# Six of the expert loads split by rows: 112 rows and twice 8 rows in place of 128

## The reference, cut to what matters

```python
def expert_block(args):
    xb, e = args
    gate, up = jnp.split(xb @ w_gate_up[e], 2, axis=-1)
    return (jax.nn.silu(gate) * up) @ w_down[e]
```

## Time and profile before

| | before |
|---|---|
| device time, median of 3 runs | 1189.67 us (1188.84 to 1191.55) |
| device time of the profiled execution | 1190.5 us |
| its span | 1189.2 us |
| PE busy | 1054.2 us, 89% |
| VectorE, ScalarE, GpSimd busy | 576.2, 479.2, 86.5 us |
| moved by DMA | 330.31 MB, mean 278 GB/s |

### The profile page before, as it was taken

How to read it: one execution, slowest core, us unless ns; L and a number is a source line. 1 busy time by engine, 2 the same in 40 slices (tenths; PEclk the granted TensorE clock), 3 DMA queues, 4 the chain that set the end, 5 groups by cost and what they waited for, 6 DMA issues and landing times.

```text
span 1189.2 us, 21996 instructions
## 1 busy us (share of the span) xinstructions
PE 1054.2 (89%) x9608; PEld 861.8 (72%) x9608; DVE 576.2 (48%) x843; ACT 479.2 (40%) x652; POOL 86.5 (7%) x91
## 2 busy tenths in 40 slices
PE   9999999996676665566678999999999999999998
PEld 8889998663333333333324899999999999999986
DVE  6765777441212121212124676664454548666643
ACT  6655953221111111111124743443357765544433
POOL 0621001000000000000000400000210004000000
PEclk9999999998778889888887999999999999999999
DMA  9843589999999999999999576454534235665520
GB/s 364 320 165 137 188 325 420 401 419 428 427 428 425 427 428 427 427 428 415 429 425 382 174 233 209 156 185 160 190 111 144 90 107 186 222 212 182 183 97 35
DMA packets 104222, 330.31 MB, mean 278 GB/s; under 512 B 4339, under 2 KB 76332, under 8 KB 86334
## 3 DMA queue, kind: packets, MB, share of 16 engines
q1 hardware_dynamic: 102064, 322.77, 70.3%
q10 hardware_dynamic: 1470, 4.02, 0.9%
q0 software_dynamic: 592, 2.10, 0.5%
HBM read 327.82 MB, written 1.06 MB: 277 GB/s over the span
## 4 chain that ended last, share of the span: by engine, by line
PE 66%; DMA 29%; DVE 2%; ACT 2%; issue 1%; SPq 0%; DVEq 0%; ACTq 0%
DMA wide<-in_w_gate_up_dram 18%; PE PS L489 13%; PE PS L490 13%; PE PS L491 13%; DMA wide<-in_w_down_dram 11%; PE PS L1229 5%; PE PS L858 4%; PE PS L504 2%; PE PS L852 2%; PE PS L505 2%; PE PS L506 2%; PE PS L1385 1%; PE PS L838 1%; DMA raw<-in_w_in_dram 1%; PE PS L1162 1%
## 5 line engine op out<-in xcount | busy, mean ns | idle before, releaser
L1992 DVE TENSOR_TENSOR lo<-raw,hi 128x2048 fp32r<-128x2048 f32 (+1 forms) x111 | 253.2, 2285 | 147.3 <-ACT hi L1477 118.8
L1477 ACT CAST hi<-raw 128x2048 fp32r<-128x2048 f32 (+1 forms) x109 | 204.0, 1875 | 111.1 <-PE PS L491 74.3
L489 PE MATMUL PS<-AH,hi 128*128 128x256 f32 (+1 forms) x816 | 232.3, 285 | 1.0 <-DVE AL L2496 1.0
L490 PE MATMUL PS<-AL,hi 128*128 128x256 f32 (+1 forms) x816 | 229.9, 282 | 0.0
L491 PE MATMUL PS<-AH,lo 128*128 128x256 f32 (+1 forms) x816 | 229.8, 282 | 0.0
L858 PE MATMUL PS<-wide,XS 128*32 128x256 f32 x1568 | 129.2, 486 | 81.9 <-DMA wide<-in_w_gate_up_dram 79.8
L858 PEld LDWEIGHTS PS<-wide,XS 128*32 128x32 f32 x1568 | 56.3, 133 | 142.6 <-DMA wide<-in_w_gate_up_dram 98.3
L489 PEld LDWEIGHTS PS<-AH,hi 128*128 128x128 f32 x816 | 153.7, 188 | 2.3 <-issue 1.0
L490 PEld LDWEIGHTS PS<-AL,hi 128*128 128x128 f32 x816 | 153.7, 188 | 0.4
L491 PEld LDWEIGHTS PS<-AH,lo 128*128 128x128 f32 x816 | 153.7, 188 | 0.0
L2424 DVE TENSOR_TENSOR Y<-PS,Y 32x256 fp32r<-32x256 f32 x128 | 53.9, 421 | 123.1 <-ACT Y L1689 120.1
(11 more groups left out here) (447 smaller groups left out, 1845.1 us busy)
## 6 DMA issues: line engine op xcount, KB each, us to landing
wide<-in_w_gate_up_dram SPq DMA_DIRECT2D x49, 2048.0 KB, 45.5
wide<-in_w_down_dram SPq DMA_DIRECT2D x25, 2048.0 KB, 45.5
raw<-in_ffn_w_gate_dram SPq DMA_DIRECT2D x22, 1024.0 KB, 5.6
raw<-in_ffn_w_up_dram SPq DMA_DIRECT2D x22, 1024.0 KB, 5.7
raw<-in_w_in_dram SPq DMA_DIRECT2D x21, 1024.0 KB, 8.4
raw<-in_ffn_w_down_dram SPq DMA_DIRECT2D x19, 1024.0 KB, 4.9
spare<-in_w_gate_up_dram SPq DMA_DIRECT2D x14, 1024.0 KB, 14.4
raw<-in_sb_w_qkv_dram SPq DMA_DIRECT2D x12, 1024.0 KB, 5.1
```

Source lines behind the costliest of these rows:

```text
L489: pe.matmul(o, w(h, c), xh(k), start=start and c == c0, stop=False)
L490: pe.matmul(o, w(h, c), xl(k), start=False, stop=False)
L1477: act.copy(K.view(K.hi[i % HN], 0, [[1, n]]), K.view(K.rbuf[i], 0, [[1, n]])).then_inc(S.hi, 1)
L1992: r = e.tensor_tensor(K.view(K.lo[i % HN], 0, [[1, n]]), K.view(K.rbuf[i], 0, [[1, n]]), K.view(K.hi[i % HN], 0, [[1, n]]).bitcast(F32), A ...
```

## The change

Every twelfth wide load, beginning with the fourth, is sent as three DMAs instead of one: rows 0 to 111, rows 112 to 119 and rows 120 to 127 of the same 128 partitions, from the same source. That makes six of the 74. All three add to the slot's semaphore, so the count for which PE waits goes up by 48 instead of 16. Slots, order, waits and every other load stay as they are.

```diff
-    K.fours = {}
+    K.fours, K.uneven = {}, {}
...
             if (i - E0) % 2 == 0:
 
-                count[lower] = count.get(lower, 0) + 1
+                K.uneven[i] = (i - E0 - TWICE) // 2 % 12 == 3
+                count[lower] = count.get(lower, 0) + (3 if K.uneven[i] else 1)
                 K.fours[i] = fours(i)
...
 def sp_two(sp, K, S, i):
 
     sp.wait_ge(S.unit, K.slot_before[i] + 1)
-    sp.dma_start(K.view(K.rbuf[i], 0, [[1, 4096]]), K.fours[i]).then_inc(S.by[K.filled[i][0]], 16)
+    filled = S.by[K.filled[i][0]]
+    for p0, rows in ((0, 112), (112, 8), (120, 8)) if K.uneven[i] else ((0, 128),):
+        sp.dma_start(K.view(K.rbuf[i], 0, [[1, 4096]], p0, rows), K.fours[i][p0:p0 + rows, :]).then_inc(filled, 16)
```

## The result

The changed kernel takes **1269.49 us** (median; 1267.83 to 1272.37) against 1189.53 of the kernel before on the same chip: a ratio of 1.0674, 95% interval 1.0661 to 1.0687. That is slower by 80 us where 20 were forecast, and far outside the range of 1188 to 1222. The profiled execution's span grew from 1189.2 to 1269.8 us. In the changed kernel `sp_two` issues at L2864, and PE's lines are one higher: L858 became L859, L852 became L853.

A forecast was written before the change was run, and what follows sets the result against it. The prediction took the wide-load stage to be bound by DMA at about 428 GB/s, the rest by compute. Issues at nothing, bytes between -3.67 and +3.67 and placement +20 us on 1190.5 gave 1210 us against the median, range 1188 to 1222.

The forecast's parts named there:

- The bound: Wide-load stage: PE waits for DMA at 427 to 428 GB/s; what its last wait gains or loses, the program does.
- Issues at nothing: SP queue: 12 more issues of 0.33 us, 4 us in all, cost nothing because transfers stay queued ahead.
- Bytes, between -3.67 and +3.67: Six split units: eight engines get 9 rows, eight get 7; between -3.67 and +3.67 us at the stage's end.
- Narrow rows, +20: 8-row DMAs into neighbouring partitions in the full stream: +20 us, taken between 11 and 31; placement decides, chance 0.63.
- `MT`'s dip: Rate dip while 16 rows of 4 KB load into partitions 0 to 15: 0.68 us per row beside its own bytes.
- How the 112 rows lie on the engines: Six units' 112-row DMAs: rows may cross into partitions another engine writes; left open, nothing added.
- upper end of +31: Top of the placement term over the six units, 36.4 - 5.6 us, meant to carry the 112 rows' open cost.
- the port rule that the prediction did cite: SBUF writes: four neighbouring partitions share one port, so four 16 KB rows queue 2.4 us where each alone takes 0.61.
- Long steps at the six units: Sign of being right: PE's starts step about 4.9 us except at or just behind the six units, not given back.
- Some 3 to 5 us too long: Sign of being right: size of the excess in PE's step at each of the six split units.
- Windows under 400 GB/s with busy engines: Sign of being right: at the six units the rate dips below 400 GB/s with DMA engines still busy.
- All three rivals: Narrow rows free: late engines get 9 rows, 1193.3 (0.11); get 7, 1186.0 (0.10); or 1188 to 1191.5 (0.16).

The follow-up runs named there:

- Experiment 1: Changed kernel with the six units split by columns into three DMAs of all 128 rows each: 1189.98 us, ratio 1.0002.
- experiment 10: Kernel before plus eight 8-row DMAs of 8 KB rows to every fourth partition behind each of five whole units: 1202.61 us, ratio 1.0113.
- experiment 11: Kernel before plus 512 KB as one 128-row DMA behind each of five whole units: 1195.61 us, ratio 1.0051.
- Experiment 5: Changed kernel with five units sent as the two 8-row DMAs alone, their first 112 rows left out: 1188.04 us, ratio 0.9988.
- experiment 6: Kernel before plus four 8-row DMAs of 8 KB rows to neighbouring partitions behind each of five whole units: 1207.41 us, ratio 1.0145.
- experiment 7: Kernel before plus four 8-row DMAs of 8 KB rows to every fourth partition behind each of five whole units: 1195.59 us, ratio 1.0048.
- experiment 2: Changed kernel with the six units sent as 112 rows and one DMA of 16 rows: 1242.4 us, ratio 1.0435.
- experiment 4: Changed kernel with five units sent as their 112 rows alone, the last 16 rows left out: 1232.64 us, ratio 1.0353.
- experiment 3: Changed kernel with the six units sent as two DMAs of 64 rows: 1239.83 us, ratio 1.0414.
- experiment 12: Changed kernel with 64 + 64 rows in six wide loads directly one behind the other, 16th to 21st: 1221.92 us, ratio 1.0273.

## Why the prediction was wrong, point by point

**The bound: right.** PE waits for the conveyor, and what the last wide load loses the program loses: +80.3 us in the stage, +80.6 in the span.

**Issues at nothing: right in effect, wrong on the issue itself.** Experiment 1 has the same twelve further issues at a ratio of 1.0002. But SP's issues, 0.33 us before, took far longer. Tile `wide` of the changed kernel (issue ns min/median/max, and us to landing), and then the gate/up issues of experiment 1:

```profile
L2864 SPq DMA_DIRECT2D wide<-in_w_gate_up_dram x61: 272/1438/11922, 251.5 to 688.2; - x61
...
DMA to landing us min/median/max: 25.8/54.2/63.8
```

```profile
L2864 SPq DMA_DIRECT2D wide<-in_w_gate_up_dram x61: 327/434/12800, 251.6 to 608.9; - x61
```

Up to 11.9 us for one issue, and 12.8 in experiment 1, where the transfers are at full rate. The least time to landing, 25.8 us, shows that the queue never drained, so it cost nothing.

**Bytes, between -3.67 and +3.67: the sign is plus** (experiments 10 and 11).

**Narrow rows, +20: about right in size, in part for another reason.** Experiment 5 gives 6 x 3.9 = 23.4 us with the bytes' 3.67 in it, some 20 without. The step from `MT`'s dip held too: 0.68 us per 4 KB row makes 1.36 per 8 KB row; experiment 6 beyond experiment 7 has 11.9 us over 5 x 32 rows, x 16 engines = 1.19 us per row. But `MT` is one DMA of 16 rows, and the same 16 rows sent as one DMA (experiment 2) cost next to nothing: +52.7 in all, where the 112 rows alone make 6 x 8.6 = 51.6. So the price belongs to the two 8-row DMAs, which put two rows on each of eight engines, and not to neighbouring partitions alone; that the sum came out near was partly luck.

**The step that failed** is the one that I did not size: "How the 112 rows lie on the engines is open as well; each engine's seven may cross into partitions that another engine writes. I add nothing for it and let the upper end carry it." It is about 55 of the 80 us (experiment 4). The question was asked and the answer put at zero, and an upper end of +31 cannot carry it. It could have been bounded from the same rows as the narrow ones: if a narrow row disturbs whoever writes beside it, then 112 rows on other engines than before are seven times as many disturbers; two engines at a time on each group of partitions is half rate, +4.9 us per unit, +29 over six, and with the narrow rows +50. That bound alone would have moved the forecast to some 1240.

The Trainium skill had the piece that was missing ("DMA: Bandwidth & Descriptors", "The descriptor swizzle"): in a load of 128 partitions each engine writes one port of its own. Read with the port rule that the prediction did cite, this would be why the whole units run at 428 GB/s: no two engines meet. That another number of rows leaves this arrangement is inferred from the rates here. The half rate of experiments 3 and 12 (209, 218 GB/s) agrees with the Trainium skill ("SBUF — State Buffer", "Door 1: The DMA port swizzle"), which gives an asymptote of some 218 GB/s for loads that reach 8 of 16 ports; that two such loads together do hardly better is what the Trainium skill says in "SBUF — State Buffer", "Can I just issue two DMAs to hit both halves?", and experiment 3 bears it out. The agreement is with the half rate alone: 16-row pieces, at 194 GB/s, did not fall to a quarter.

**What remained of the rest.** By half rate for two units each, six lone 112-row loads would add 54 us, and experiment 4 makes it 6 x 8.6 = 52. The lag in the timeline is uneven, though: the start that answers to 316.60 is this one in the timeline of PE in the kernel before:

```profile
306.64 3.52 PE L858 MATMUL PS<-wide,XS 128*32 128x256 f32 x32 [2.96 <-DMA wide<-in_w_gate_up_dram]
```

So behind the first split unit PE is 9.96 us later, less the 0.87 by which it started later (277.92 against 277.05): 9.1 us. The mean of six is 80.3 / 6 = 13.4. Around the fourth, steps of about 10 us begin two units ahead of it. The fifth alone adds 16.6 us. Its start in the changed kernel, and the one that answers to it in the kernel before:

```profile
597.15 3.64 PE L859 MATMUL PS<-wide,XS 128*32 128x256 f32 x32 [8.50 <-DMA wide<-in_w_gate_up_dram]
```

```profile
529.76 1.93 PE L858 MATMUL PS<-wide,XS 128*32 128x256 f32 x32 [1.60 <-DMA wide<-in_w_gate_up_dram]
```

Taken the same way, PE is 66.5 us behind here, where the fourth was 49.9 us behind (521.76 against 470.94). The engines drift further apart with each odd unit. From the first to the last raise of a whole load's semaphore (as in experiment 10) it is 3.5, 7.6, 11.7 and 18.2 us behind the first four split units of the changed kernel, where the kernel before has 2.9, 4.2, 4.5 and 5.7 at the same places and the 112 + 16 rows of experiment 2 have 3.5, 3.6, 5.2 and 5.9. So it is the two 8-row DMAs that drive the engines apart. That more whole units therefore meet the split one is argued: the units of experiment 4 grow dearer too, while this spread only goes from 3.0 to 7.5 us there.

**What was to show it.** Long steps at the six units and not given back: yes. "Some 3 to 5 us too long": no, 9 and more, spread over two and more units. Windows under 400 GB/s with busy engines: yes, and much deeper. All three rivals needed the narrow rows to be free, and experiment 6 shows that neighbouring ones are not.

**Open:** which rows of a DMA with fewer than 128 rows go to which engine, which engines by number are the late ones, and by what rule two engines share partitions. No view shows an engine by its number. That the 112 and the 64 rows are slow for the reason that experiments 6 and 7 show, the partitions, is inferred: their own cost is measured, but no run sends so many rows to scattered partitions, and a split by rows also changes which source rows are read at once.

## What to carry to other kernels

When a stream of whole 128-partition loads runs at its limit, cut a load by columns, which cost nothing here, and not by rows, which halved the rate for the load and for one whole neighbour or more. When a change touches how data lies on parallel engines, size the largest part of the data first, also where its cost seems open: a bound of "twice as slow for as long as it lasts" is better than zero. Read GB/s beside the busy share: the engines counted as 100% busy at half the rate.

## What the runs showed that I had not expected

- Rows in every fourth partition went through a full stream at 431 GB/s, the same rows in neighbouring partitions (of the other half) at 283.
- Seven slow steps for six split units in a row: loads that are whole pay for one that is not.
- Halves, quarters and eighths of a unit by rows cost alike, 8.4, 9.2 and 9.5 us per unit.
- SP's issue of one DMA lasted up to 11.9 us, and 12.8 in experiment 1, where it cost nothing; before, the longest of the gate/up loads was 3.5.
- Two 8-row DMAs drive the engines apart for the rest of the stage: the raises of one whole load's semaphore lay 18.2 us apart behind four split units, 5.7 in the kernel before.
